# Latent value products of twelve heads as three products of rounded and remaining parts, with the values moved behind the scores, and a token scale and an entry reordered

## The chip, the core and the metric

The kernel runs on one core of one Trainium2 chip. The metric is the device time of one execution in microseconds (us). Engines: PE (TensorE: MATMUL, with its weight loads shown as PEld), DVE (VectorE), ACT (ScalarE), POOL (GpSimd), SP (SyncE, which issues the DMAs). Each works through its own queue in order; semaphores join them.

## What is computed

A transformer of three layers over 512 tokens of width 1024, in float32. The first layer mixes gated linear attention, sliding-window attention and causal pooling, then a feed-forward block. The second has a causal attention of 16 heads of 64 ("fox") and a feed-forward block. The third has latent attention of 16 heads of 128 ("mla") and a feed-forward block. The change touches the token scale at the entry of fox, and latent attention, cut here to what matters:

```python
def mla_shared_kv(x, kv_in_g, w_dkv, kv_norm_g, w_uk, w_uv, cos, sin):
    ckv = rmsnorm_2(x, kv_in_g) @ w_dkv
    latent = rmsnorm_2(ckv[..., :KV_LORA], kv_norm_g)          # 256 wide
    k_rope = apply_rope(ckv[..., KV_LORA:], cos, sin)
    k_nope = (latent @ w_uk).reshape(b, s_len, MLA_HEADS, 128)
    v = (latent @ w_uv).reshape(b, s_len, MLA_HEADS, 128)

def mla_mixer(h, w_dq, q_norm_g, w_uq, w_out, k_nope, k_rope, v, cos, sin):
    q = (rmsnorm_2(h @ w_dq, q_norm_g) @ w_uq)                 # 768 -> 16 x (128 + 64)
    ...
        sc = (qn . k_nope + qr . k_rope) * scale               # masked by chunks of 64 tokens
        p = jax.nn.softmax(sc, axis=-1)
        return jnp.einsum('bhqk,bkhd->bqhd', p, v)             # the value product of the title
    return o.reshape(b, s_len, 16 * 128) @ w_out
```

## The kernel before

**Weights.** All weights come as 380 chunks of up to 8 blocks of 128 columns. SP fetches chunk c into slot c mod 4 once PE has finished chunk c-4 (`fetch`, L539). ACT rounds it to fp32r (`casts`, L1276, WHI), POOL subtracts to get the remainder (L595, WLO), and PE makes each product of three passes of fp32r: WHI with the rounded input, WHI with the remainder of the input, WLO with the rounded input (`split_mm`, L603 to L605; by tokens `token_part`, L688 to L690). `part` and `group` run such a product into one PSUM bank. `bank_free` makes the first matmul of a group wait until the group that had the bank before was drained by DVE (semaphore `drained`).

**Order.** Each engine's order is written out by hand: the same step (`mla_pair`, `fox_pair`) stands once in the PE block, once in ACT's and once in DVE's. `linear_plan` gives the order of the chunks, and `bank_table` derives the banks from it, two banks taking turns for most groups.

**A latent pair p** (heads a = 2p and b = 2p+1, for p = 0 to 6). PE: scores of a and b (`mla_scores`, L1163 masks and L1173 products); `qr.p+1` (rotary queries) and `qn.a+2` (queries), 18 matmuls each; `turn` of a (10 transposes, L1053); for p > 0 the values `mv` (24 matmuls of 256 columns); the keys `kn.a+2` and `kn.b+2` (6 matmuls each); `mla_weigh` of a (L1062: probabilities by values, in full fp32, over 512, 384, 256 and 128 columns); turn of b; `qn.b+2`; weigh of b. ACT: the exponentials, the casts, the copy of the turned probabilities to MPT (`copy_turned`, L1561), the rounded parts of queries and keys, the rounded output. DVE: row maxima and scaling of the probabilities (L2167, L2178); the rope, that is the drain of `qr` to QRS, RT, four TURNED and the sum RT (L1752, L1749, L2345); the drain of `qn.a+2` to QNF; those of values and keys; the remainders; the output's remainder.

**Entry of latent attention.** PE: `kn.0`, `kn.1`, the sum of squares for the query norm (`stats("qn", 6)`, L712), `qr.0`, `qn.0`, `qn.1`, `mv0`, then the pairs.

**Token scales.** `stats` multiplies ones with SUMSQ over 512 columns (L712) and ACT makes RSTD by Ln and Exp (`root`). Two sites (`mixpost`, `ffnpost`) do otherwise: `token_sums` (L717, matmuls of 1 column), a square root of 4 columns on ACT (`deviation`), a reciprocal on DVE, and `spread` (L724) with filling matmuls (`keep_clock`, L731) around it. Fox has `stats` in the middle of its value products (before the third row block of k = 6), `root`, and a turn of RSTD to columns (`by_token_scale`, L758), after which DVE drains FV.

## Time and profile before

| | |
|---|---|
| median of 3 runs | 2189.12 us (2186.57 to 2189.54) |
| the profiled execution: its time | 2188.44 us |
| its span | 2186.6 us (1.8 us lie around it) |
| PE, PEld busy | 2166.6 (99%), 1774.1 (81%) |
| DVE, ACT, POOL busy | 1218.9 (56%), 898.5 (41%), 967.9 (44%) |
| mean granted clock of TensorE | 0.997 of full speed |
| DMA | 191.76 MB, 27.9% of 16 engines |

Busy times are sums over the whole span. A matmul's duration includes the time it takes to drain; what one costs in a stream is the distance from its start to the next one's. "idle before, releaser" gives how long an engine stood still before an instruction, and whose end let it go.

### The profile page before, as it was taken

The page shows a single profiled execution, that of the slowest core. Times are in us where ns is not written, and L with a number is a line of the kernel's source. Part 1 is how long each engine was busy: PE and PEld are TensorE (multiplying, and loading weights), DVE is VectorE, ACT ScalarE, POOL GpSimd, SP SyncE. Part 2 cuts the span into 40 slices and gives each one's busy share as a digit, 9 for nine tenths or more (in the row PEclk, how much of TensorE's full clock was granted, in tenths as well). Part 3 has the DMA queues.
Part 4 walks back from the last instruction along what each step waited for, and adds up shares of the span by engine and source line. Part 5 has one row for each costly group of instructions (what it writes and reads, how often), then busy time and mean ns, then how long its engine had stood idle before and what let it go on. Part 6 is the DMA issues. An engine that isn't in the chain of part 4 may idle for free.

```text
span 2186.6 us, 26205 instructions
## 1 busy us (share of the span) xinstructions
PE 2166.6 (99%) x10422; PEld 1774.1 (81%) x10422; DVE 1218.9 (56%) x1713; ACT 898.5 (41%) x1406; POOL 967.9 (44%) x741
## 2 busy tenths in 40 slices
PE   9999999999999999999999999999999999999998
PEld 6887788878888887777888888887888888888887
DVE  4975424478995136775566661177666425666511
ACT  5224422354343234675533332265444434333322
POOL 4434335545565444321554444444222344444442
PEclk9999999999999999999999999999999999999999
DMA  5222222323333323111333323332111133333332
GB/s 183 78 68 68 73 83 95 104 90 97 97 97 93 98 76 99 60 57 58 97 97 97 97 94 97 99 94 68 56 54 54 58 106 97 97 97 97 94 98 89
DMA packets 59097, 191.76 MB, mean 88 GB/s; under 512 B 6592, under 2 KB 8800, under 8 KB 58976
## 3 DMA queue, kind: packets, MB, share of 16 engines
q1 hardware_dynamic: 58976, 190.09, 27.9%
q8 instruction: 83, 1.36, 0.3%
q14 instruction: 38, 0.31, 0.0%
HBM read 187.96 MB, written 2.10 MB: 87 GB/s over the span
## 4 chain that ended last, share of the span: by engine, by line
PE 92%; DVE 5%; ACT 1%; DMA 1%; issue 1%; SPq 0%; DVEq 0%; ACTq 0%
PE ps L603 26%; PE ps L604 26%; PE ps L605 26%; PE ps L1173 2%; PE ps L1062 1%; PE ps L1053 1%; PE ps L688 1%; PE ps L689 1%; PE ps L690 1%; DVE TURNED L1749 1%; PE ps L1122 1%; DMA RAW<-weights 1%; PE ps L1091 1%; PE ps L780 1%; DVE SUMSQ L1765 1%
## 5 line engine op out<-in xcount | busy, mean ns | idle before, releaser
L595 POOL TENSOR_TENSOR WLO<-RAW,WHI 128x512 fp32r<-128x512 f32 (+1 forms) x733 | 966.3, 1343 | 1185.0 <-ACT WHI L1276 1183.0
L1276 ACT ACTIVATE WHI<-RAW 128x1024 fp32r<-128x1024 f32 (+3 forms) x379 | 374.1, 989 | 683.9 <-DMA RAW<-weights 486.5
L603 PE MATMUL ps<-HH,WHI 128*128 128x512 f32 x1194 | 470.7, 394 | 0.0
L604 PE MATMUL ps<-HL,WHI 128*128 128x512 f32 x1194 | 465.0, 389 | 0.0
L605 PE MATMUL ps<-HH,WLO 128*128 128x512 f32 x1194 | 465.0, 389 | 0.0
L1752 DVE SCALAR_TENSOR_TENSOR CV<-U,PAR,CV 128x512 f32<-128x512 f32 x264 | 301.9, 1161 | 27.0 <-ACT CV L1524 22.0
L603 PEld LDWEIGHTS ps<-HH,WHI 128*128 128x128 f32 x1194 | 224.3, 188 | 50.9 <-issue 3.8
L604 PEld LDWEIGHTS ps<-HL,WHI 128*128 128x128 f32 x1194 | 224.3, 188 | 47.9 <-issue 2.2
L605 PEld LDWEIGHTS ps<-HH,WLO 128*128 128x128 f32 x1194 | 224.2, 188 | 46.8
L603 PE MATMUL ps<-ACTH,WHI 128*128 128x512 f32 (+1 forms) x550 | 209.4, 381 | 0.0
L604 PE MATMUL ps<-ACTL,WHI 128*128 128x512 f32 (+1 forms) x550 | 209.3, 381 | 0.0
L605 PE MATMUL ps<-ACTH,WLO 128*128 128x512 f32 (+1 forms) x550 | 209.3, 381 | 0.0
L1749 DVE TENSOR_TENSOR U<-ps,RSTD 128x512 f32<-128x512 f32 x132 | 89.0, 686 | 176.6 <-PE ps L605 164.5
L2137 DVE TENSOR_TENSOR X<-X,ps 128x512 f32<-128x512 f32 x31 | 21.2, 685 | 226.1 <-PE ps L605 226.1
L1524 ACT ACTIVATE CV<-U,PAR 128x512 f32<-128x512 f32 x132 | 106.3, 807 | 88.2 <-DVE U L1749 88.2
L603 PE MATMUL ps<-HUH,WHI 128*128 128x512 f32 x352 | 137.3, 390 | 0.0
L605 PE MATMUL ps<-HUH,WLO 128*128 128x512 f32 x352 | 137.0, 389 | 0.0
L604 PE MATMUL ps<-HUL,WHI 128*128 128x512 f32 x352 | 136.9, 389 | 0.0
L605 PEld LDWEIGHTS ps<-ACTH,WLO 128*128 128x128 f32 x550 | 103.4, 188 | 19.9
L603 PEld LDWEIGHTS ps<-ACTH,WHI 128*128 128x128 f32 x550 | 103.4, 188 | 19.9
L604 PEld LDWEIGHTS ps<-ACTL,WHI 128*128 128x128 f32 x550 | 103.4, 188 | 19.5
L1765 DVE TENSOR_TENSOR SUMSQ<-SUMSQ,SQ 128x512 f32<-128x512 f32 x77 | 74.1, 962 | 19.9 <-ACT SQ L1310 19.3
(344 smaller groups left out, 3260.1 us busy)
## 6 DMA issues: line engine op xcount, KB each, us to landing
RAW<-weights SPq DMA_DIRECT2D x288, 512.0 KB, 3.5
RAW<-weights SPq DMA_DIRECT2D x56, 384.0 KB, 3.0
RAW<-weights SPq DMA_DIRECT2D x29, 256.0 KB, 2.6
RAW<-weights SPq DMA_DIRECT2D x8, 320.0 KB, 2.9
outT<-X SPq DMA_DIRECT2D x8, 256.0 KB, 2.2
X<-xT SPq DMA_DIRECT2D x3, 512.0 KB, 8.5
X<-xT SPq DMA_DIRECT2D x2, 256.0 KB, 4.0
RESET<-resets SPq DMA_DIRECT2D x1, 512.0 KB, 9.4
```

The costliest lines, as they stand in the source:

```text
L595: pool.tensor_tensor(WLO[:, slot, w], RAW[:, slot, w], WHI[:, slot, w].bitcast(F32), ALU.subtract).then_inc(w_lo, 1)
L603: pe.matmul(out, wh, hh, start=first, stop=False)
L604: pe.matmul(out, wh, hl, start=False, stop=False)
L605: return pe.matmul(out, wl, hh, start=False, stop=last)
L688: pe.matmul(o, hi[k][:, q], WHI[:, slot, w], start=k == 0, stop=False)
L689: pe.matmul(o, lo[k][:, q], WHI[:, slot, w], start=False, stop=False)
L1173: mm = pe.matmul(ps[:, 2 + 3 * odd + bank, col:col + length], q_[:, i * P:(i + 1) * P], k_[:, 0:length], start=False, stop=m == len(produc ...
L1276: act.activation(WHI[:, slot, 0:cols], RAW[:, slot, 0:cols], ACT.Copy).then_inc(w_hi, 1)
L1524: act.activation(CV[:, m, :], U[:, m, 2:2 + T], ACT.Identity, bias=par(f"conv{f}", at + 3), scale=par(f"conv{f}", at + 2)).then_inc(tap, 1)
L1749: return dve.tensor_tensor(out, a, b, ALU.mult)
L1752: return dve.scalar_tensor_tensor(out, a, scalar, b, op0, op1)
L1765: dve.tensor_tensor(SUMSQ[:, :], SUMSQ[:, :], SQ[:, slot, :], ALU.add).then_inc(sumsq, 1)
```

## The change

It does five things. (1) For pairs 0 to 5 (SPLIT_PAIRS = 6, heads 0 to 11) the value product is `split_weigh`: for the first three key blocks three fp32r passes (MVH with MPTH, MVL with MPTH, MVH with MPTL), for the last one an fp32 product (MPTF with MV). ACT writes MPTH and MPTF in the place of MPT, and MVH once a pair (`values_hi`); DVE subtracts MVL once a pair (`values_lo`) and MPTL once a head (`turned_lo`). (2) The values `mv` of pairs 1 to 6 move from behind turn(a) to behind the scores, on all engines; they get a chunk of their own, so that a pair has five chunks where it had four. (3) Fox gets the token scale by `token_sums`, `deviation` and `spread`, with the sums later, before the second row block of k = 7. (4) `token_sums` multiplies with 128 columns of ones in the place of one, at all its sites, and the readers take every 128th column. (5) At the entry of latent attention `qr.0` and the sum come ahead of the keys, and the rope is made before the scale is known and scaled afterwards.

```diff
@@ linear_plan
+    whole("qr.0", QLORA_K)
     add(("kn.0", "kn.0", 0, LORA_K), ("kn.1", "kn.1", 0, LORA_K))
-    for name in ("qr.0", "qn.0", "qn.1"):
+    for name in ("qn.0", "qn.1"):
         whole(name, QLORA_K)
...
         a, b = 2 * p + 2, 2 * p + 3
+        if p:
+            tokens([f"mv{p}.{half}" for half in range(2)], f"mv{p}", 0, 2 * LORA_K)
         if p < MLA_H // 2 - 1:
             whole(f"qr.{p + 1}", QLORA_K)
             whole(f"qn.{a}", QLORA_K)
-        values = [(f"mv{p}.{half}", f"mv{p}", 0, 2 * LORA_K, 0) for half in range(2)] if p else []
...
+            add((f"kn.{a}", f"kn.{a}", 0, LORA_K), (f"kn.{b}", f"kn.{b}", 0, LORA_K))
             whole(f"qn.{b}", QLORA_K)
@@ PE
-                    mm = pe.matmul(ps[:, bank, col + n:col + n + 1], squares[:, b * P:(b + 1) * P], ones[:, 0:1],
+                    mm = pe.matmul(ps[:, bank, col + n * P:col + (n + 1) * P], squares[:, b * P:(b + 1) * P], ones,
...
-                    if k == KD - 2 and r == 2:
-                        stats("fox", 8)
+                    if k == KD - 1 and r == 1:
+                        pe.wait_ge(sumsq, SQ_AT["fox"] + KD + 2)
+                        token_sums(7, 0, SUMSQ, range(NT), True, True).then_inc(stat_done, 1)
...
-                        by_token_scale("fox")
+                        pe.wait_ge(inverted, 1 + SITES_BY_TOKEN.index("fox"))
+                        spread(7, range(NT)).then_inc(rstd_done, 1)
...
+            def split_weigh(n):
+
+                out, own = ps[:, 4 + 3 * (n % 2), :], slice(n % 2 * P, n % 2 * P + P)
+                pe.wait_ge(a_pt, (n + FOX_H) * 3 + 3)
+                pe.wait_ge(mv_lo, n // 2 + 1)
+                pe.wait_ge(turned_lo_done, n + 1)
+                for j in range(NT - 1):
+                    bank, col, length = COLS[j]
+                    at = slice(bank * T + col, bank * T + col + length)
+                    pe.matmul(out[:, j * P:T], MVH[:, j, own], MPTH[:, at], start=j == 0, stop=False)
+                    pe.matmul(out[:, j * P:T], MVL[:, j, own], MPTH[:, at], start=False, stop=False)
+                    pe.matmul(out[:, j * P:T], MVH[:, j, own], MPTL[:, at], start=False, stop=False)
+                pe.matmul(out[:, (NT - 1) * P:T], MV[:, NT - 1, own], MPTF[:, :], start=False, stop=True).then_inc(a_o, 1)
@@ mla_pair on PE
                 mla_scores(b)
+                if p:
+                    mla_values(p)
                 group(f"qr.{p + 1}", *CQ_)
                 group(f"qn.{a + 2}", *CQ_)
                 mla_turn(a)
-                if p:
-                    mla_values(p)
                 group(f"kn.{a + 2}", *L_)
                 group(f"kn.{b + 2}", *L_)
-                mla_weigh(a)
+                weigh_head(a)
@@ ACT
-            root("fox", D, RSTD)
+            deviation("fox", D, 7)
             casts(chunk_of("fv1.0", 2))
+            act.wait_ge(rstd_done, STAT_AT["fox"] + 1)
+            act.activation(RSTD[:, :], ps[:, 7, :], ACT.Copy).then_inc(row_done, 1)
...
+            def values_hi(p):
+                product(f"mv{p}.1")
+                act.activation(MVH[:, 0:NT - 1, :], MV[:, 0:NT - 1, :], ACT.Copy).then_inc(mv_hi, 1)
@@ DVE
+            def values_lo(p):
+                dve.wait_ge(mv_hi, p + 1)
+                dve.tensor_tensor(MVL[:, 0:NT - 1, :], MV[:, 0:NT - 1, :], MVH[:, 0:NT - 1, :].bitcast(F32), ALU.subtract
+                                  ).then_inc(mv_lo, 1)
+            def turned_lo(n):
+
+                for b, length in enumerate((T, 3 * P, 2 * P)):
+                    dve.wait_ge(a_pt, (n + FOX_H) * 3 + b + 1)
+                    at = slice(b * T, b * T + length)
+                    last = dve.tensor_tensor(MPTL[:, at], ps[:, 2 + 3 * (n % 2) + b, 0:length], MPTH[:, at].bitcast(F32),
+                                             ALU.subtract)
+                last.then_inc(turned_lo_done, 1)
@@ mla_pair on DVE
                 rotated(p + 1)
+                if p < SPLIT_PAIRS:
+                    values_lo(p)
                 drain_q(a + 2)
-                if p:
-                    drain_values(p, 0)
-                    drain_values(p, 1)
+                if p < SPLIT_PAIRS:
+                    turned_lo(a)
                 drain_k(a + 2)
@@ entry on PE and on DVE
-            pe.wait_ge(lat_done, LORA_K)
+            group("qr.0", *CQ_, (lat_done, LORA_K))
+            pe.wait_ge(col_read, 2)
+            stats("qn", 6)
             group("kn.0", *L_)
             group("kn.1", *L_)
-            pe.wait_ge(col_read, 3)
-            stats("qn", 6)
-            group("qr.0", *CQ_, (lat_done, LORA_K))
...
+            dve.tensor_scalar(QRS[:, :], ps[:, BANK["qr.0"], :], MLA_SCALE, None, ALU.mult).then_inc(drained, 1)
...
+            rope(dve.tensor_tensor(RT[:, :], TURNED[:, :], RT[:, :], ALU.add))
```

In a pair of the first six the order now is, on PE, scores a and b, mv, qr, qn, turn(a), kn twice, weigh(a), turn(b), qn, weigh(b). How the instructions stand at the three places that matter is shown here (names as in the program; x is a count, waits are semaphores).

PE, the first value product of pair 1 (heads 2 and 3), before:

```order
L605 MATMUL ps<-LH,WLO 128x512
L1062 MATMUL ps<-MPT,MV 128x512 [waits a_pt,drained]
L1062 MATMUL ps<-MPT,MV 128x384
L1062 MATMUL ps<-MPT,MV 128x256
L1062 MATMUL ps<-MPT,MV 128x128
L1053 MATMUL ps<-CON,MP 128x128 [waits a_p]
```

and now:

```order
L616 MATMUL ps<-LH,WLO 128x512
L1208 MATMUL ps<-MPTH,MVH 128x512 [waits turned_lo_done,mv_lo,a_pt]
L1209 MATMUL ps<-MPTH,MVL 128x512
L1210 MATMUL ps<-MPTL,MVH 128x512
L1208 MATMUL ps<-MPTH,MVH 128x384
L1209 MATMUL ps<-MPTH,MVL 128x384
L1210 MATMUL ps<-MPTL,MVH 128x384
L1208 MATMUL ps<-MPTH,MVH 128x256
L1209 MATMUL ps<-MPTH,MVL 128x256
L1210 MATMUL ps<-MPTL,MVH 128x256
L1211 MATMUL ps<-MPTF,MV 128x128
L1064 MATMUL ps<-CON,MP 128x128 [waits a_p]
```

Four fp32 products became nine fp32r products and one fp32 product, and they wait for two more semaphores, both counted up by DVE.

DVE, pair 1, from the drain of the rotary queries on, before:

```order
L1752 SCALAR_TENSOR_TENSOR QRS<-ps,RSTD 128x512 [waits lin_done,m_rot]
L1749 TENSOR_TENSOR RT<-QRS,CS 128x512 [waits drained]
L1749 TENSOR_TENSOR TURNED<-QRS,CS 32x512 x4
L2345 TENSOR_TENSOR RT<-TURNED,RT 128x512 [waits m_dve]
L1752 SCALAR_TENSOR_TENSOR QNF<-ps,RSTD 128x512 [waits lin_done]
L1749 TENSOR_TENSOR MV<-ps,RCOL 128x512 [waits lin_done] x2
L1749 TENSOR_TENSOR KNF<-ps,RSTDK 128x512 [waits lin_done] x2
L2352 TENSOR_TENSOR QRHL<-RT,QRHL 64x512 [waits rope_hi]
L2352 TENSOR_TENSOR QRHL<-RT,QRHL 64x512
```

and now:

```order
L1802 SCALAR_TENSOR_TENSOR QRS<-ps,RSTD 128x512 [waits lin_done,m_rot]
L1799 TENSOR_TENSOR RT<-QRS,CS 128x512 [waits drained]
L1799 TENSOR_TENSOR TURNED<-QRS,CS 32x512 x4
L2397 TENSOR_TENSOR RT<-TURNED,RT 128x512 [waits m_dve]
L2413 TENSOR_TENSOR MVL<-MV,MVH 128x768 [waits mv_hi]
L1802 SCALAR_TENSOR_TENSOR QNF<-ps,RSTD 128x512 [waits lin_done]
L2421 TENSOR_TENSOR MPTL<-ps,MPTH 128x512 [waits a_pt]
L2421 TENSOR_TENSOR MPTL<-ps,MPTH 128x384 [waits a_pt]
L2421 TENSOR_TENSOR MPTL<-ps,MPTH 128x256 [waits a_pt]
L1799 TENSOR_TENSOR KNF<-ps,RSTDK 128x512 [waits lin_done] x2
L2404 TENSOR_TENSOR QRHL<-RT,QRHL 64x512 [waits rope_hi]
L2404 TENSOR_TENSOR QRHL<-RT,QRHL 64x512
```

The two drains of MV are gone from here (they stand behind the row maxima now); MVL stands ahead of the drain to QNF, and three MPTL stand ahead of the drains to KNF.

PE, the keys of the same pair, now (before, the second group waited for `mv1.1`, which DVE drains after QNF):

```order
L614 MATMUL ps<-LH,WHI 128x512 [waits w_lo,drained]
L615 MATMUL ps<-LL,WHI 128x512
L616 MATMUL ps<-LH,WLO 128x512
L614 MATMUL ps<-LH,WHI 128x512
L615 MATMUL ps<-LL,WHI 128x512
L616 MATMUL ps<-LH,WLO 128x512
L614 MATMUL ps<-LH,WHI 128x512 [waits drained]
L615 MATMUL ps<-LL,WHI 128x512
L616 MATMUL ps<-LH,WLO 128x512
L614 MATMUL ps<-LH,WHI 128x512
L615 MATMUL ps<-LL,WHI 128x512
L616 MATMUL ps<-LH,WLO 128x512
```

The first row of the second group waits for `drained`, and by the table of banks the group that had this bank is `qn.4`, whose drain is the QNF above.

## Rows read from the trace of the kernel before

**Rows 1.** The page: engines, and one group of weight loads

```profile
PE 2166.6 (99%) x10422; PEld 1774.1 (81%) x10422; DVE 1218.9 (56%) x1713; ACT 898.5 (41%) x1406; POOL 967.9 (44%) x741
...
L603 PEld LDWEIGHTS ps<-HH,WHI 128*128 128x128 f32 x1194 | 224.3, 188 | 50.9 <-issue 3.8
```

**Rows 2.** PE's timeline at mixpost's and fox's sums: start us, us, engine, line, operation

```profile
435.15 0.95 PE L717 MATMUL ps<-CON,SUMSQ 128*128 128x1 f32 x8
...
830.71 0.39 PE L690 MATMUL ps<-WLO,HH 128*128 128x512 f32 x1
833.25 1.28 PE L712 MATMUL ps<-SUMSQ,CON 128*128 128x512 f32 x2 [2.15 <-DVE SUMSQ L1765]
...
842.75 1.05 PE L758 MATMUL ps<-CON,RSTD 1*128 1x1 f32 x8
```

**Rows 3.** Windows, three stretches: busy us, then granted clock, DMA share, GB/s

```profile
834.10:837.30 3.20, 3.20 (x8) 2.32 (x7) 0.00 (x0) 3.17 (x3) 2.70 (x3) 0.50 0.01 3
438.30:441.60 3.30, 3.30 (x13) 1.87 (x12) 1.80 (x4) 0.23 (x1) 0.00 (x0) 0.51 0.00 0
1492.70:1494.30 1.60, 0.00 (x0) 0.00 (x1) 1.60 (x2) 1.49 (x2) 1.60 (x2) 1.00 0.31 101
```

**Rows 4.** PE's timeline at the entry of latent attention

```profile
1476.45 1.10 PE L712 MATMUL ps<-SUMSQ,CON 128*128 128x512 f32 x2 [0.77 <-DVE SUMSQ L1765]
...
1494.30 0.29 PE L1163 MATMUL ps<-M 128*128 128x64 bf16 x4 [1.60 <-DVE QNL L2322]
```

**Rows 5.** The chain that ended last, one value product (start us, us)

```profile
1639.59 2.16 PE ps L1062 x8
```

**Rows 6.** PE's timeline, scores of a latent head

```profile
1559.53 0.40 PE L1173 MATMUL ps<-KRL,QRHL 128*128 128x512 f32 x1
1559.76 0.34 PE L1173 MATMUL ps<-KNH,QNH 128*128 128x384 f32 x1
1559.94 0.34 PE L1173 MATMUL ps<-KNH,QNL 128*128 128x384 f32 x1
...
1561.21 0.28 PE L1173 MATMUL ps<-KNH,QNL 128*128 128x256 f32 x1
1561.33 0.28 PE L1173 MATMUL ps<-KNL,QNH 128*128 128x256 f32 x1
```

**Rows 7.** PE's timeline in pair 0: turn(a), kn.a, kn.b, weigh(a)

```profile
1509.05 1.25 PE L1053 MATMUL ps<-CON,MP 128*128 128x128 f32 x10
1510.06 0.48 PE L603 MATMUL ps<-LH,WHI 128*128 128x512 f32 x1
...
1511.97 0.50 PE L603 MATMUL ps<-LH,WHI 128*128 128x512 f32 x1 [0.27 <-DVE QNF L1752]
...
1513.47 1.02 PE L1062 MATMUL ps<-MPT,MV 128*128 128x512 f32 x2
```

**Rows 8.** Timelines of DVE, POOL, ACT and PE in pair 3

```profile
1628.58 0.69 DVE L1752 SCALAR_TENSOR_TENSOR QRS<-ps,RSTD 128x512 f32<-128x512 f32 x1 [0.94 <-PE ps L605]
...
1632.82 1.66 DVE L2345 TENSOR_TENSOR RT<-TURNED,RT 128x512 f32<-128x512 f32 x1
1634.40 0.68 DVE L1752 SCALAR_TENSOR_TENSOR QNF<-ps,RSTD 128x512 f32<-128x512 f32 x1
...
1632.44 2.64 POOL L595 TENSOR_TENSOR WLO<-RAW,WHI 128x512 fp32r<-128x512 f32 x2 [10.80 <-ACT WHI L1276]
...
1631.52 0.85 ACT L1276 ACTIVATE WHI<-RAW 128x768 fp32r<-128x768 f32 x1 [5.49 <-DMA RAW<-weights]
1633.03 1.36 ACT L1561 ACTIVATE MPT<-ps 128x512 f32<-128x512 f32 x3 [0.67 <-PE ps L1053]
...
1632.39 1.25 PE L1053 MATMUL ps<-CON,MP 128*128 128x128 f32 x10
```

**Rows 9.** The page: DMA issues, KB each, us to landing

```profile
RAW<-weights SPq DMA_DIRECT2D x56, 384.0 KB, 3.0
RAW<-weights SPq DMA_DIRECT2D x29, 256.0 KB, 2.6
```

More of the change, by code:

```diff
@@ L165, in linear_plan @@
             whole(f"qn.{a}", QLORA_K)
-        values = [(f"mv{p}.{half}", f"mv{p}", 0, 2 * LORA_K, 0) for half in range(2)] if p else []
-        if p < MLA_H // 2 - 1:
-            values += [(f"kn.{n}", f"kn.{n}", 0, LORA_K, (4 + 2 * (n - a)) * P) for n in (a, b)]
-        chunks.append(values)
-        if p < MLA_H // 2 - 1:
+            add((f"kn.{a}", f"kn.{a}", 0, LORA_K), (f"kn.{b}", f"kn.{b}", 0, LORA_K))
             whole(f"qn.{b}", QLORA_K)
@@ L408, in on_chip_model @@
         TURNED = nc.alloc_sbuf_tensor_at("TURNED", [P, T], F32, offset=sumsq_at)
+        mpt_at = mol_at + MLA_H * T * 4
+        MPTH = over("MPTH", [P, 5 * 2 * P], mpt_at, F32R)
+        MPTL = over("MPTL", [P, 5 * 2 * P], mol_at + 2 * SPLIT_PAIRS * T * 4, F32R)
+        MPTF = over("MPTF", [P, P], mol_at + (2 * SPLIT_PAIRS + 3) * T * 4)
+        MVH = over("MVH", [P, NT, 2 * P], hh_at + 2 * SPLIT_PAIRS * T * 4, F32R)
+        MVL = over("MVL", [P, NT, 2 * P], hh_at + (2 * SPLIT_PAIRS + 2) * T * 4, F32R)
         CKV = nc.alloc_sbuf_tensor_at("CKV", [P, LORA_K, T], F32, offset=mol_at)
@@ L500, in on_chip_model @@
         SITES = list(STAT_AT)
-        SITES_BY_TOKEN = ("mixpost", "ffnpost")
+        SITES_BY_TOKEN = ("mixpost", "ffnpost", "fox")
         def par(name, at=0, n=1):
@@ L1499, in _ @@
                 fb_square("wout", j, "mixpost")
-            deviation("mixpost", D)
+            deviation("mixpost", D, 6)
             for j in range(KD):
@@ L1537, in _ @@
             casts(chunk_of("fv0.0", 2))
-            deviation("ffnpost", D)
+            deviation("ffnpost", D, 6)
             for j in range(KD):
@@ L1644, in _ @@
                 square(j, (SQ_AT["qn"] + j) % 2, CQ[:, j, :], "qn")
+            casts(chunk_of("qn.1"))
             root("qn", QLORA_K * P, RSTD)
+            casts(chunk_of("mv0.0"))
             def query_hi(n):
@@ L1706, in _ @@
             key_hi(1)
-            casts(chunk_of("mv0.0"))
             rotated_hi(0)
@@ L2179, in normalise @@
                 last.then_inc(a_p, 1)
-            scale_known("fox")
-            col_scale(2)
+            dve.wait_ge(ln_done, STAT_AT["fox"] + 1)
+            dve.reciprocal(RCOL[:, :], RCOL[:, :]).then_inc(inverted, 1)
+            dve.wait_ge(inverted, 1 + SITES_BY_TOKEN.index("fox"))
             for r in range(NT):
                 drain_rows(f"fv0.{r}", FV[:, r, 0:512], r, RCOL)
+            dve.wait_ge(row_done, 1)
             drain("foxf", FZ[:, 0, :])
@@ L2361, in mla_softmax @@
                     row_maxima(2 * p + h + FOX_H, h, 2 + 3 * h)
+                if p:
+                    drain_values(p, 0)
+                    drain_values(p, 1)
                 for h in range(2):
@@ L2384, in mla_pair @@
                 head_out(b)
+            dve.wait_ge(lin_done, DONE["qr.0"])
+            dve.tensor_scalar(QRS[:, :], ps[:, BANK["qr.0"], :], MLA_SCALE, None, ALU.mult).then_inc(drained, 1)
+            dve.wait_ge(drained, DRAIN["qr.0"])
+            mul(RT[:, :], QRS[:, :], CS[:, 0, :])
+            dve.wait_ge(stat_done, STAT_AT["qn"] + 1)
+            rope(swapped(TURNED, range(4)))
+            rope(dve.tensor_tensor(RT[:, :], TURNED[:, :], RT[:, :], ALU.add))
             scale_known("kvn")
@@ L2389, in _ @@
             scale_known("qn")
-            drain_rope(0)
-            rope(swapped(TURNED, range(4)))
-            rotated(0)
+            mul(RT[:, :], RT[:, :], RSTD[:, :]).then_inc(m_rot, 1)
             drain_q(0)
+            key_lo(0)
+            key_lo(1)
+            rotated_lo(0)
+            query_lo(0).then_inc(head_ready, 1)
             drain_q(1)
-            rotated_lo(0)
-            key_lo(0)
-            query_lo(0).then_inc(head_ready, 1)
-            key_lo(1)
             query_lo(1).then_inc(head_ready, 1)
```

37 lines of the change are left out of this document (30 added, 7 removed).

## The prediction

> **What bounds the kernel now.** I read the page first: PE is busy 99% of the span [rows 1]. So the time is the length of PE's queue plus the few places where PE stands still or runs at the lower clock, and a change is worth what it takes from that queue less what it makes PE wait. Next I read PE's own rows for its waits and the windows for the granted clock. Three places stand out. At the end of fox's first value half, the row block before ends, then the sum over SUMSQ waits 2.15 us for DVE [rows 2], and right behind it the granted clock is 0.50, that is 1.2 in place of 2.4 GHz, for 3.2 us [rows 3]. Another stretch at 0.51 follows the one-column matmuls of the mixpost site [rows 3]. The entry of latent attention has waits of 0.77 and 1.60 us [rows 4]; there the clock stayed at 1.00 [rows 3]. In the latent pairs PE hardly waits; what matters there is how much room DVE has, so last I read the rows of DVE, ACT and POOL in one pair.
>
> The sum is made against the profiled execution, 2188.4 us; the median of the runs, 2189.1, is 0.7 above.
>
> **The passes.** A value product takes 2.16 us of PE [rows 5]. In a stream, start to start, an fp32r pass costs 0.23 us over 512 columns, 0.18 over 384 and 0.12 over 256 [rows 6]. Three of each are 1.59, and the fp32 product over 128 of the 1280 columns, a tenth of 2.16, is 0.22: 1.81, or about 1.9 with the start of a new stream. That is 0.3 us less a head, 0.6 a pair, and 3.6 for twelve heads.
>
> **What waits for the new parts.** Count from the start of turn(a). The turn takes 1.01 and each key group 1.5 or less: in pair 0 the turn starts at 1509.05, kn.a at 1510.06, and kn.b at 1511.97 because it waits for QNF, and weigh starts 1.50 later [rows 7]. Without that wait a key group is six passes of 0.23, 1.4, so kn.b could begin at 2.4 and weigh(a) at 3.8. Now look at DVE in pair 3, where turn(a) starts at 1632.39: QRS starts 3.8 earlier, the sum of the rope ends at 2.1, QNF at 2.7 [rows 8]. Before, PE covered this with the values, some 3.1 us of work between turn and keys. They have moved away, and kn.b now waits for QNF in every pair, as in pair 0.
>
> Ahead of QNF stands MVL, 768 columns from SBUF. No row has it: the least is 0.69, a subtraction of 512, the most 1.04, that in proportion; I take 1.0. Behind QNF stand three MPTL of 512, 384 and 256 columns: 0.69 and in proportion 0.52 and 0.35, together 1.5 to 1.6. ACT is no limit: MPT was complete 2.0 after the turn's start [rows 8], and one more small copy makes that 2.3.
>
> How late the rope ends depends on POOL. The rope's last step took 1.66 us where POOL's WLO was running, against the 0.69 of QRS before it. QNF, which reads PSUM, took 0.68 beside the same WLO [rows 8]. In pair 3 the rope was held once, by 0.97; without that it ends at 1.1. Now two chunks come at it. The values free their chunk 8.0 before turn(a) (36 passes of 0.23 lie between), the 384 KB take 3.0 [rows 9], the cast 0.85 [rows 8], and POOL starts near -4.1, one us ahead of RT: I price this hold at 0.8. The rotary queries end at -3.95, their successor is now the 256 KB of the next values, 2.6 [rows 9] and a cast of 0.6, so POOL starts near -0.65, in the middle of TURNED: 1.0. The rope ends at 2.9, MVL at 3.9, QNF at 4.6, kn.b starts at 4.65 and ends at 6.0, MPTL is there at 6.15. Weigh(a) starts at 6.2 in place of 3.8: **a wait of 2.4 us in each of pairs 1 to 5**, against 0.6 gained. The bounds: no hold at all gives QNF at 2.8 and MPTL at 4.4, a wait of 0.6; holds of 1.0 and 1.5 give 3.1. I take 2.4, by the times at which the two chunks land.
>
> The Trainium skill (SBUF — State Buffer, "SBUF: two separate sides") says that a DVE operation with two SBUF inputs and a GpSimd operation that reads SBUF exclude each other for a whole instruction. By that rule MVL, with two SBUF inputs, can be held by a third piece of WLO as well, and the five pairs would be up to 5 us longer; the three MPTL, with one input in PSUM, could not. The trace agrees as far as it goes: 1.66 for the first kind, 0.68 for the second.
>
> Pair 0 has its values ahead of the pairs, so only the second hold: rope 2.1 to 2.5, weigh(a) at 5.7, while before it was at 4.4 [rows 7]: +1.3, less 0.6, is +0.7. Pairs 1 to 5: 5 x (2.4 - 0.6) = +9.0. Pair 6 has no new parts but the new order: QNF at 3.6, kn.b 1.2 late: +1.2. Weigh(b) has room: turn(b) and qn.b are 5.2 us of cover behind weigh(a), in which DVE has five drains and remainders of 0.7, the output's remainder and 1.6 for MPTL; I cost it at nothing, and if this cover is gone it is up to 0.8 a pair. The last pair is as before.
>
> **Clock in the pairs.** PE stands still in front of kn.b from 2.4 to 4.65, 2.25 us. The nearest rows are the wait of 2.15 that was followed by 1.2 GHz and the one of 1.60 that was not [rows 2, 3, 4]. A fall that lasts 3.2 us costs 1.6. Five such waits: none to five falls, 0 to 8 us. I take one, 1.6: the wait of 2.15 had its fall, but a single row doesn't make it a rule for all five.
>
> **Fox.** The sum moves behind k = 6 and the first row block of k = 7. That is twelve more passes, 2.7 us, and DVE's last square let the sum go 2.3 after the block before it: the wait goes, with 0.4 to spare, and with it the low clock behind it. From 830.94, where the next pass would have started, to 842.75 the rows show 11.81 us [rows 2]. The work in it is 30 passes of 0.2275 and the sum, 2.16 x 512 / 1280 = 0.86, together 7.7. So **-4.1 us**. The sum itself keeps its size (four fp32 products of 128 columns for one of 512). Spread, eight matmuls of 128 columns, takes the place of the turn to columns, eight of 1 column; both are 0.8 to 1.0 by the rows of the next part. The square root, the reciprocal and ACT's copy of the row lie beside fv1; DVE's drains begin earlier than before, so nothing is late there.
>
> **Mixpost, ffnpost, final.** Four fp32 products of 1 column, eight matmuls, took 0.95 [rows 2]; ten transposes of 128 columns take 1.01 [rows 7], so eight matmuls of 128 are 0.8 and a little, the same within 0.1. But behind the one-column groups at mixpost the clock was 0.51 for 3.3 us, half of which is 1.65 lost [rows 3]. With full columns in that stretch I expect the clock to hold. Since PE may then wait for its first input tile, I take -1.0 (0 to -1.65). The final site adds 0.1.
>
> **Entry.** Putting qr.0 first lets the last squares finish under it, and the rope starts 4.7 us earlier and no longer holds up the first head. Both waits of rows 4 go, 0.77 + 1.60. The first pass stood at 1472.8 (twelve passes end where the wait of 0.77 begins). The longest chain left is qn.0 (48 passes and the sum later, 1484.6), QNF, the rounded part, two KNL, two QRHL, QNL, 4.5 us, against the end of mv0 at 1491.9: cover 2.7, by which even two holds fit. **-2.4.**
>
> **Sum.** Fox -4.1, mixpost -1.0, final +0.1, entry -2.4, pairs +0.7 +9.0 +1.2, clock +1.6: +5.1, so 2193.5 against the profiled time and **2194 against the median**. A measurement of this kernel can tell about 0.2%, 4.4 us, from no change.
>
> **Rivals.**
> - *DVE is in time* (faster). If WLO misses the rope, weigh(a) waits 0.6 at most, the pairs give nothing away, and the gains outside remain: -7.4 and -1 at most, 2180 to 2182. It decides at MPTL complete 3.8 to 4.4 us after the turn starts. For it: in pair 3 QRS, RT and TURNED ran unheld, and only the last step met WLO. Against: the chunk that the values free is timed to land just ahead of RT. 14%.
> - *One hold a pair* (no change): a wait of 1.4, pairs +4 to +5, total -3: 2185 to 2188. The case if a landing is 0.8 us earlier or later than I reckon. 26%.
> - *The clock falls in most pairs*, or MVL is held too (slower): 8 us for five falls in place of 1.6, or 5 for MVL: 2199 to 2203. 15%.
> - *The passes aren't cheaper*, because each has its own weight load of 0.188 [rows 1] and costs no less: then 384 and 256 columns cost 0.19, a product 2.1, and the gain of 3.6 goes. The rows show 0.12 for passes with a new weight each [rows 6], so I give it 3% and leave it in the range.
> - My forecast has 42%, with a range of its own of 2189 to 2199.
>
> **How the numbers follow.** The range of 2181 to 2203 leaves out the lower half of the first rival and a little above the third. Faster by over 0.2% is below 2184.7: the first rival and a part of the second, 0.20. Within 0.2%: the rest of the second and the lower part of the forecast, 0.34. Slower: 0.46.
>
> **What would show it.** PE's row of kn.b in each of the first seven pairs should have an idle time before it that ends with QNF, 1 to 3 us; weigh(a) should follow MPTL; TURNED or RT should be longer than 0.69 in most pairs. Value products should take 1.8 to 1.9. Fox's sum should start without a wait, with a clock of 1.00 behind it, and the stretch behind mixpost's sums should be at 1.00 too. The first scores should follow mv0 at once. The forecast is wrong if kn.b starts within 1 us of kn.a's end, or if mixpost's clock stays low.

## The result and the profile after

The changed kernel takes 2190.1 us (median of 20 runs, 2188.1 to 2191.8) where the kernel before took 2187.1 in the same comparison (20 runs, 2185.2 to 2191.2). The ratio is 1.0013 with a 95% interval of 1.0007 to 1.0019: 3 us slower, inside the predicted range, and less than the 5 of the forecast. By the bound of 0.2% that the prediction set, it counts as no change, which had 0.34; slower by more than that had 0.46.

The engines on the page of the profiled execution (span 2188.4, against 2186.6 before) answer to [rows 1]; the second block is PE's waits over the latent pairs (line waited at, releaser: us in total, times, longest):

```profile
PE 2161.8 (99%) x10464; PEld 1777.3 (81%) x10464; DVE 1246.3 (57%) x1756; ACT 902.7 (41%) x1429; POOL 966.9 (44%) x740
```

```profile
PE ps L614 <- DVE QNF L1802: 11.4, 7, 2.4
PE ps L1176 <- DVE MOL L2408: 1.4, 2, 0.8
PE ps L1208 <- DVE MPTL L2421: 0.7, 1, 0.7
```

PE is busy 4.8 us less and the program is longer all the same. The seven waits at L614 are kn.b in the first seven pairs. A wait costs some 0.3 more than the idle time shown: in pair 2 the value product starts 5.70 after the turn, and with nothing to wait for (experiment 11) 3.84, which is 1.86 later for an idle time of 1.57. The idle time is counted from the drained end of the last pass, and the first pass of a new stream takes longer. PE's timeline in pair 2 shows one of them, and a split value product behind it:

```profile
1566.65 1.26 PE L1064 MATMUL ps<-CON,MP 128*128 128x128 f32 x10
...
1568.90 0.39 PE L616 MATMUL ps<-LH,WLO 128*128 128x512 f32 x1
1570.86 0.50 PE L614 MATMUL ps<-LH,WHI 128*128 128x512 f32 x1 [1.57 <-DVE QNF L1802]
...
1572.35 0.47 PE L1208 MATMUL ps<-MPTH,MVH 128*128 128x512 f32 x1
...
1574.22 1.26 PE L1064 MATMUL ps<-CON,MP 128*128 128x128 f32 x10
```

The product takes 1.87 from its start to that of the next turn, against 2.16 before [rows 5]. DVE and POOL in the same stretch:

```profile
1562.83 0.69 DVE L1802 SCALAR_TENSOR_TENSOR QRS<-ps,RSTD 128x512 f32<-128x512 f32 x1 [0.69 <-PE ps L616]
1563.56 0.81 DVE L1799 TENSOR_TENSOR RT<-QRS,CS 128x512 f32<-128x512 f32 x1
1564.38 4.22 DVE L1799 TENSOR_TENSOR TURNED<-QRS,CS 32x512 f32<-32x512 f32 x4
1568.64 0.69 DVE L2397 TENSOR_TENSOR RT<-TURNED,RT 128x512 f32<-128x512 f32 x1
1569.25 0.95 DVE L2413 TENSOR_TENSOR MVL<-MV,MVH 128x768 fp32r<-128x768 f32 x1
1570.12 0.68 DVE L1802 SCALAR_TENSOR_TENSOR QNF<-ps,RSTD 128x512 f32<-128x512 f32 x1
1570.72 1.48 DVE L2421 TENSOR_TENSOR MPTL<-ps,MPTH 128x512 fp32r<-128x512 f32 x3
...
1562.53 2.43 POOL L606 TENSOR_TENSOR WLO<-RAW,WHI 128x512 fp32r<-128x512 f32 x2 [11.56 <-ACT WHI L1303]
1566.08 1.28 POOL L606 TENSOR_TENSOR WLO<-RAW,WHI 128x512 fp32r<-128x512 f32 x1 [1.12 <-ACT WHI L1303]
```

DVE goes without a gap from QRS to the last MPTL. Two pieces of POOL's work lie on it: the first stretches RT and one TURNED step, the second another TURNED step, so that the four take 4.22. QNF comes 4.15 after the turn's start, kn.b at once behind it, and the value product at 5.7, right after the third MPTL (1572.20).

Windows of the granted clock, to be read against [rows 3] (us, busy times, then clock, DMA share, GB/s): behind mixpost's sums, at fox's sum, and behind kn.b in pair 4.

```profile
434.90:442.40 7.50, 7.05 (x42) 4.75 (x42) 4.49 (x8) 2.10 (x4) 0.77 (x2) 1.00 0.16 52
829.00:842.00 13.00, 13.00 (x67) 11.03 (x66) 8.60 (x13) 5.48 (x8) 9.02 (x8) 1.00 0.41 122
1637.30:1640.70 3.40, 3.40 (x10) 2.65 (x11) 2.89 (x6) 2.00 (x6) 1.10 (x2) 0.59 0.02 4
```

Both low stretches of before are gone, and a new one stands behind the longest wait, 2.39 us in pair 4. The first scores of the latent stage start at 1485.62 instead of 1494.30 [rows 4]: **8.7 us gained by then**, about 2.6 of it because the trace of before has the two low stretches (experiment 1). The scores of the last pair start at 1713.41 instead of 1711.65: **the pairs took 10.4 back**. From scores to scores the seven pairs before the last cost +0.8, +1.8, +1.2, +1.9, +3.1, +1.3 and +0.3.

### The profile page after: what moved, and what is told of

Read it like the earlier page. It is cut to its first block, busy times and chain, and to the rows that moved or that the text cites. A ratio compares the mean times of both kernels' runs of the same rounds, so it can differ in the third digit from the quotient of the medians.

```text
span 2188.4 us, 26359 instructions
## 1 busy us (share of the span) xinstructions
PE 2161.8 (99%) x10464; PEld 1777.3 (81%) x10464; DVE 1246.3 (57%) x1756; ACT 902.7 (41%) x1429; POOL 966.9 (44%) x740
## 4 chain that ended last, share of the span: by engine, by line
PE 93%; DVE 4%; DMA 1%; ACT 1%; issue 0%; SPq 0%; POOL 0%; DVEq 0%; ACTq 0%
PE ps L614 26%; PE ps L616 26%; PE ps L615 26%; PE ps L1186 2%; PE ps L699 1%; DVE TURNED L1799 1%; PE ps L700 1%; PE ps L701 1%; DMA RAW<-weights 1%; PE ps L1064 1%; PE ps L1135 1%; PE ps L1104 1%; PE ps L791 1%; PE ps L1073 0%; PE ps L865 0%
## 5 line engine op out<-in xcount | busy, mean ns | idle before, releaser
L614 PE MATMUL ps<-HH,WHI 128*128 128x512 f32 x1194 | 470.6, 394 | 0.6 <-POOL WLO L606 0.6
L614 PEld LDWEIGHTS ps<-HH,WHI 128*128 128x128 f32 x1194 | 224.2, 188 | 51.6 <-issue 3.8
L614 PE MATMUL ps<-ACTH,WHI 128*128 128x512 f32 (+1 forms) x550 | 209.5, 381 | 0.0
L614 PE MATMUL ps<-HUH,WHI 128*128 128x512 f32 x352 | 137.3, 390 | 0.0
L614 PEld LDWEIGHTS ps<-ACTH,WHI 128*128 128x128 f32 x550 | 103.4, 188 | 19.6
```

The lines of the kernel that those rows point to most:

```text
L614: pe.matmul(out, wh, hh, start=first, stop=False)
```

## The experiments

The kernels were timed in three groups of four; the median of before was 2186.2, 2187.1 and 2187.7 beside them. So each kernel is compared by its ratio to the before of its own group. A ratio's interval is about 2 us to either side (up to 3 where a kernel ran five or six times), and a difference of two ratios is less sure than that.

**1. The two parts outside the pairs, each alone.** First the fox token scale with the wide sums on the kernel before:

```
-                    if k == KD - 2 and r == 2:
-                        stats("fox", 8)
+                    if k == KD - 1 and r == 1:
+                        pe.wait_ge(sumsq, SQ_AT["fox"] + KD + 2)
+                        token_sums(7, 0, SUMSQ, range(NT), True, True).then_inc(stat_done, 1)
...
-            root("fox", D, RSTD)
+            deviation("fox", D, 7)
...
```

> The kernel before with only the change's token scale of the fox layer and its 128-column sums (the reader's view of them too); pairs and entry as before. My theory: the fox part gives 4.1 and mixpost 1.0 (one full clock instead of the throttled stretch), so 2187.1 - 5.1 = 2182 (range 2180.5 to 2184), with the granted clock 1.00 at both places. Rival, that what came out after was made elsewhere: fox sums queued later give only the matmul's own time back, under 2, and the run stands at 2185 or above.

Measured: 2182.7, ratio 0.9982 (0.9974 to 0.9991), about 4 us faster. Then the entry alone, PE's part shown (ACT's and DVE's orders follow it):

```
...
-            pe.wait_ge(lat_done, LORA_K)
+            group("qr.0", *CQ_, (lat_done, LORA_K))
+            pe.wait_ge(col_read, 3)
+            stats("qn", 6)
             group("kn.0", *L_)
             group("kn.1", *L_)
-            pe.wait_ge(col_read, 3)
-            stats("qn", 6)
-            group("qr.0", *CQ_, (lat_done, LORA_K))
...
```

> The kernel before with only the new entry of the latent stage (rotary product first, statistics behind it, queries' rest ordered anew). My theory: the waits of 0.77 and 1.60 ahead of the first scores go, so 2187.1 - 2.4 to 2.8 = 2184.5 (range 2183.3 to 2186). Rival: the gain of the entry comes only with the shorter product of the split values behind it, then the run stands at 2186.5 or above.

Measured: 2184.0, ratio 0.9989 (0.9980 to 0.9997). Its trace has no wait at the entry, and from the first pass of the stage to the first scores it takes 18.73 us (1470.16 to 1488.89), where the run with the old entry takes 21.49: 2.75 gained. It also shows something on the fox part, which is as before in this kernel. PE's row of fox's sum, and the windows behind it and behind mixpost's one-column sums:

```profile
832.30 0.70 PE L713 MATMUL ps<-SUMSQ,CON 128*128 128x512 f32 x1 [2.17 <-DVE SUMSQ L1766]
...
438.30:441.60 3.30, 2.92 (x17) 1.47 (x16) 2.26 (x5) 0.83 (x2) 0.00 (x0) 1.00 0.00 0
832.30:835.50 3.20, 3.20 (x12) 2.32 (x13) 0.00 (x0) 3.03 (x3) 3.01 (x3) 1.00 0.01 3
```

The same wait and the same one-column groups stand there, and the clock stays at 1.00. So the two low stretches of [rows 3] come in some executions and not in others. The times of before say so too: over 64 of its executions beside these runs the median is 2185.8 where the mean clock was 0.999, 2187.0 at 0.998 and 2187.9 at 0.997. At full clock the fox part alone is worth 2.7: the same pass of the stage behind it starts at 859.24 in the run with it and at 861.71 in the run without, while ahead of the sum the run with it is 0.2 behind (824.75 and 824.52). Mixpost was at full clock in both. Another 0.4 comes by the end of fox's pairs; what it comes from was not looked into.

**2. Both parts together, the pairs untouched** (the two diffs above in one kernel).

> The kernel before with both parts of the change that lie outside the pairs (fox token scale with the 128-column sums, and the latent entry), the pairs untouched. If the parts are independent: 2186.2 - 3.5 - 2.3 = 2180.4 (range 2179 to 2182), which would be below both kernels, and the change's pairs then cost the difference to the changed kernel, 9. If they overlap (the fox part's gain and the entry's both being the same clock stretch or the same wait), 2182.5 or more.

Measured: 2179.9, ratio 0.9969 (0.9958 to 0.9981), 6.8 faster. They add up (0.18% + 0.11% = 0.29%, against 0.31%). So the pairs of the changed kernel cost 0.44%, 9.6 us, in timed runs (11 by the traces, 1.5 of it the low clock in pair 4).

**3. No head split, all else as changed.**

```
-SPLIT_PAIRS = 6
+SPLIT_PAIRS = 0
```

> The changed kernel with no head's value product split: all sixteen in single fp32 passes, values still behind the scores, entry and fox changed. Theory A (the split costs DVE and GpSimd-port work in front of kn.b that eats what its passes give back): the waits ahead of kn.b stay, as the rope chain still stands there, but without the remainder of the values (0.95) and of the first turned head (1.5); they fall from 1.6 to under 0.7 a pair, and the time is 2181 to 2184, that is, below the kernel before and 6 to 9 below the changed one. Theory B (the split is a gain that the new order hides): each pair loses the 0.6 of its two cheaper products and gets no wait back: 2193 to 2195.

Measured: 2185.1, ratio 0.9995 (0.9986 to 1.0003); a point above the range of theory A and far from B. The 9.6 come apart into two: moving the values behind the scores costs 5.7 (0.9969 to 0.9995), and splitting the products costs 3.9 more (0.9995 to 1.0013). Each of the two is known to some 3 us; the traces have 6.4 and 4.5 for them, from the first scores of the stage to those of the last pair. I had expected the waits ahead of kn.b to fall below 0.7 in each pair. They are 0.6 to 1.6, and the rotary steps are still held (TURNED x4 takes 4.29 in pair 1):

```profile
PE ps L614 <- DVE QNF L1802: 6.5, 7, 1.6
```

**4. The values' remainder out of the queue.**

```
                 for h in range(2):
                     normalise(2 * p + h + FOX_H, h, MP[:, h, :])
+                if p < SPLIT_PAIRS:
+                    values_lo(p)
...
                 rotated(p + 1)
-                if p < SPLIT_PAIRS:
-                    values_lo(p)
                 drain_q(a + 2)
```

> The changed kernel with one DVE instruction moved: the remainder of the values (128x768, 0.95 us) stands behind the probabilities' scaling instead of between the rotary sum and the query's drain. In the trace of the changed kernel DVE is idle there for about 0.7 before the rotary product comes. Theory A (the length of DVE's queue from the rotary product to the query's drain sets kn.b): the waits ahead of kn.b fall by 0.7 in each of the pairs 0 to 5, from 1.5-1.8 to 0.8-1.1, and the run stands 4 to 5 below the changed kernel, at 2184 to 2186 where the kernel before has 2186. Theory B (DVE only follows TensorE, kn.b waits for something that starts with the turned head): waits and time as in the changed kernel, 2188 to 2190.

Measured: 2185.1, ratio 0.9993 (0.9984 to 1.0001). PE's waits have 8.0 at kn.b instead of 11.4, the clock is not low in the pairs, and by the ratios it is 4.4 faster than the changed kernel:

```profile
PE ps L614 <- DVE QNF L1802: 8.0, 7, 1.9
```

Theory A holds in the pairs 1 to 5: what DVE does between QRS and QNF is paid by PE. In pair 2 QNF ends 0.53 earlier after the turn's start (3.62 for 4.15), and the wait is 0.53 shorter (1.04 for 1.57). It is not the whole 0.87 that was moved: QRS starts 0.09 later, and the first hold is longer (RT takes 1.07 in place of 0.81). In pair 0 the wait did not fall (1.88 for 1.80): there DVE has no idle time ahead of QRS, so MVL pushed the rope back by what it took away behind it.

**5. The control: another consumer first.**

```
                 rotated(p + 1)
+                drain_q(a + 2)
                 if p < SPLIT_PAIRS:
                     values_lo(p)
-                drain_q(a + 2)
```

> The changed kernel with the query's drain put ahead of the remainder of the values on DVE. A control: the same instructions in the same stretch, another consumer first. Theory A with two waits in a row (kn.b for the drained query, then the first value product for the remainder of the turned head): kn.b's waits fall by 0.95, but the value product right behind it then waits about 0.8, so that the sum of the two is as before and the time within 1 of the changed kernel (2188.5 to 2190.5). Theory B (only the wait of kn.b counts): 5 to 6 below the changed kernel, 2183 to 2185.

Measured: 2189.0, ratio 1.0013 (1.0004 to 1.0022), as the changed kernel. PE's waits:

```profile
PE ps L614 <- DVE QNF L1802: 6.2, 7, 1.6
PE ps L1208 <- DVE MPTL L2421: 5.3, 11, 0.7
```

6.2 and 5.3 are 11.5 in place of 11.4 and 0.7. Most of what left kn.b went to the value product behind it, and the time stayed: in pair 2 the turn after weigh(a) starts 7.56 after the one before it, and 7.57 in the changed kernel. kn.b and this product are asked for one right behind the other and are fed by one queue, so what counts is when the queue is through with both.

**6. GpSimd off the rotary steps.** ACT makes the rounded weights, POOL their remainders behind it. Two casts move behind the turned head's copies:

```
                 if 0 < p < SPLIT_PAIRS:
                     values_hi(p)
+                mla_turned(a)
                 if p:
                     casts(chunk_of(f"mv{p}.0") + RING)
                 casts(chunk_of(f"qr.{p + 1}") + RING)
-                mla_turned(a)
```

> The changed kernel with ACT's two weight casts (of the values' chunk and of the next rotary chunk) moved behind the turned head's copies, so that GpSimd's weight remainder, which follows them, no longer falls on DVE's rotary steps. Theory A (the shared port: two holds of 0.8 to 1.0 us on the rotary steps are what makes kn.b late): rotary steps of 0.7 each instead of up to 1.7, waits ahead of kn.b of 0 to 0.6 in place of 1.5 to 2.4 in the pairs 0 to 5, time 2190.1 - 6 to 8 = 2183 (range 2182 to 2187, the upper end if the remainder then falls on the next DVE steps). Theory B (the queue alone is too long, holds are incidental): waits shorter by under 0.4 each, time 2188 to 2190. Theory C: the later casts make a weight late on TensorE, a new wait appears ahead of a qn or kn product, and the time rises above 2190.

Measured: 2202.2, ratio 1.0075 (1.0061 to 1.0089), 13.6 slower than the changed kernel by the two ratios. Theory C had the sign, but no weight is late on TensorE, and no theory had the size. PE's waits, then DVE and POOL in pair 1:

```profile
PE ps L1208 <- DVE MPTL L2421: 18.0, 6, 3.0
PE ps L1176 <- DVE MOL L2408: 0.5, 1, 0.5
```

```profile
1533.78 2.77 DVE L1799 TENSOR_TENSOR TURNED<-QRS,CS 32x512 f32<-32x512 f32 x4
...
1541.38 3.15 DVE L2404 TENSOR_TENSOR QRHL<-RT,QRHL 64x512 fp32r<-64x512 f32 x2
1544.54 1.00 DVE L2374 TENSOR_TENSOR QNL<-QNF,QNH 128x384 fp32r<-128x384 f32 x1
1545.46 2.92 DVE L2384 TENSOR_TENSOR KNL<-KNF,KNH 128x512 fp32r<-128x512 f32 x2
1548.31 0.68 DVE L2408 TENSOR_TENSOR MOL<-ps,MOH 128x512 fp32r<-128x512 f32 x1
1548.91 1.47 DVE L2421 TENSOR_TENSOR MPTL<-ps,MPTH 128x512 fp32r<-128x512 f32 x3
...
1539.04 8.80 POOL L606 TENSOR_TENSOR WLO<-RAW,WHI 128x512 fp32r<-128x512 f32 x7 [20.96 <-ACT WHI L1303]
```

The first half of theory A is right. TURNED x4 takes 2.77 instead of 4.22, and no idle time is left ahead of kn.b in any of the seven pairs. But POOL now works in one block of 8.80, and beside it stand other steps with two operands in SBUF. QRHL x2, QNL and KNL x2 took 1.39, 0.56 and 1.28 in the changed kernel; here they take 3.15, 1.00 and 2.92, 3.8 more. The steps that read PSUM beside the same block (MOL, MPTL) keep their length. The second head's MPTL stands behind all of them, and the second value product waits 3.0 in six pairs. The clock was then low at four of the six waits, 17.1 us in all; I reckon half of it, 8.5, as lost (a little less, as 0.8 of it lies in a wait). A window over the product in pair 1:

```profile
1550.50:1554.00 3.50, 3.48 (x15) 3.14 (x16) 1.03 (x2) 1.15 (x2) 1.27 (x1) 0.53 0.00 0
```

The sum: 18.5 of waits and 8.5 of clock, less the changed kernel's 13.5 of waits and 1.7 of clock, is 11.8. The spans differ by 12.0 (2200.4 and 2188.4). The sum is rough by about 1, as each wait costs a little more than its idle time.

**7. One head's remainder moved in front of three steps.** On top of the late casts:

```
                 rotated_lo(p + 1)
                 query_lo(a + 2)
+                if p < SPLIT_PAIRS:
+                    turned_lo(b)
                 key_lo(a + 2).then_inc(head_ready, 1)
                 key_lo(b + 2)
                 head_out(a)
-                if p < SPLIT_PAIRS:
-                    turned_lo(b)
```

> The run with late casts and one edit more: the second turned head's remainder ahead of both keys' remainders on DVE; the values' remainder stays where the change put it. Theory A (the 3.0 ahead of the second value product was one step of the queue standing behind two keys' remainders of 1.8 and 1.2 and the first head's output of 0.7): the wait falls to under 0.8 and with it the clock falls that came after it, time 2176 to 2180 against 2202 with late casts alone. Theory B (both edits of the reordered kernel were needed): above 2185.

Measured: 2176.1, ratio 0.9952 (0.9939 to 0.9964). That is in theory A's range. No value product waits, and no low clock is left in the pairs. By the two ratios 27 us hung on where one head's remainder stood, some 18 of waits and 8 of clock.

**8. The same with the values' remainder early as well** (the edits of 4, 6 and 7 together).

> The run with late casts (2202.2) had no wait ahead of kn.b, but 3.0 ahead of the second value product, whose operand stood on DVE behind six remainders of operands that GpSimd's weight remainder now slowed. This kernel keeps the late casts, and on DVE puts the values' remainder behind the probabilities' scaling and the second turned head's remainder ahead of both keys' remainders and of the first head's output. Theory A (one DVE queue, GpSimd's holds fall on whatever two-SBUF-operand step stands beside them, what counts is whether TensorE's operand is in front of it or behind): both waits go, under 0.5 each pair is left, time 2202 - 6 times 2.6 to 3.0 = 2184 to 2187, about the kernel before or just below. Theory B (DVE is out of time in a pair of 33 us whatever the order): the wait comes back ahead of the next scores, and the time stays above 2192.

Measured: 2175.6, ratio 0.9952 (0.9940 to 0.9965), 8.4 below the near end of theory A's range: I had priced the waits that go, and not the 8.5 of low clock that stood behind them. Left are 1.6 us of waits for the first head's output and 0.3 for one MPTL. Against experiment 7 the early remainder of the values adds nothing that these runs can tell. The traces show why: in pair 2 turn(a), both key groups and weigh(a) are through in 5.63 in place of 5.98, because QNF ends at 1.81 and not at 2.58, where kn.b had to wait for it a little; and qn.b with weigh(b), in front of scores that wait for MOL, gives the 0.35 back (6.50 in place of 6.14).

**9. Is it the order alone?** Edits 4 and 7, but the casts as the change has them:

> The reordered kernel without the late casts: values' remainder and second turned head's remainder early on DVE, ACT's casts where the change has them, so that GpSimd's weight remainder falls on the rotary steps again. Theory A (the holds on the rotary steps set kn.b): the waits of 0.9 to 1.3 ahead of kn.b stay as in the run with the early remainder of the values (2185.1), time 2184 to 2186. Theory B (the order on DVE is all, the holds matter nowhere once it is right): 2176 to 2179.

Measured: 2184.0, ratio 0.9986 (0.9977 to 0.9995), with 8.2 us of waits ahead of kn.b (8.0 in experiment 4):

```profile
PE ps L614 <- DVE QNF L1802: 8.2, 7, 1.8
```

The holds on the rotary steps matter by themselves: 0.34%, 7.4 us, lie between this and the reordered kernel. The two edits work only as a pair: the late casts alone lose 13.6, and the second head's remainder alone gains nothing that these runs can tell (0.9993 and 0.9986, whose intervals overlap; 0.5 us by the traces of the pairs).

**10. What the three passes are worth.** The reordered kernel with SPLIT_PAIRS = 0:

> The reordered kernel (2175.6) with no head split: twelve value products go back to one fp32 pass each. It asks what the three passes are worth where TensorE waits for nothing. Theory A (0.3 less a product): no wait appears, turned head to turned head is 0.3 longer than in the split kernel, time 2175.6 + 12 x 0.3 = 2179.2 (range 2178 to 2181). Theory B (the three passes give nothing by themselves, all of the gain came with the order): 2175 to 2176.5.

Measured: 2177.2, ratio 0.9956 (0.9944 to 0.9968), less than theory A's 2179.2. Part of that is the 1.6 us of waits that only the split kernel has; experiment 11, where they are gone too, is 3.8 us below this kernel. Not all of it is the split's: by the traces 3.1 us lie in the six split pairs and 0.7 in pair 6, whose products are not split in either, and where this kernel waits 0.47 for ACT's MPT. From turn to turn a pair takes 30.99 us without the split and 30.48 with it (1530.57 to 1561.56, and 1530.78 to 1561.26), 0.5 for two products.

**11. The last waits.**

```
                 key_lo(a + 2).then_inc(head_ready, 1)
-                key_lo(b + 2)
                 head_out(a)
+                key_lo(b + 2)
                 drain_q(b + 2)
```

> The reordered kernel with the first head's output remainder ahead of the second key's remainder on DVE. Its seven waits of 0.15 to 0.43 (1.6 in all) ahead of the scores, which stood for that output, should go in the pairs 0 to 5: 2175.6 - 1.0 = 2174.6. If the wait only moves to the key's remainder, 2175.6 as before.

Measured: **2173.5**, ratio 0.9937 (0.9925 to 0.9949): 13.8 us faster than the kernel before and 16.6 faster than the change, by the ratios. It is more than the 1.0 that I had expected: by the traces of the pairs 2.7, because an idle time of 0.16 stood for a delay of 0.3, and pair 6 lost another delay of 0.6. Against the kernel with untouched pairs (experiment 2) it is 7 us less by the ratios, 5.8 by the traces. The engines on its page, its only wait in the pairs, and DVE and POOL in pair 2:

```profile
PE 2158.0 (99%) x10464; PEld 1776.6 (82%) x10464; DVE 1249.9 (58%) x1756; ACT 898.2 (41%) x1429; POOL 972.0 (45%) x740
```

```profile
PE ps L1208 <- DVE MPTL L2421: 0.2, 1, 0.2
```

```profile
1556.66 0.95 DVE L2413 TENSOR_TENSOR MVL<-MV,MVH 128x768 fp32r<-128x768 f32 x1
...
1558.95 2.77 DVE L1799 TENSOR_TENSOR TURNED<-QRS,CS 32x512 f32<-32x512 f32 x4
...
1562.97 1.48 DVE L2421 TENSOR_TENSOR MPTL<-ps,MPTH 128x512 fp32r<-128x512 f32 x3
...
1566.56 3.06 DVE L2404 TENSOR_TENSOR QRHL<-RT,QRHL 64x512 fp32r<-64x512 f32 x2 [0.57 <-ACT QRHL L1693]
...
1570.56 1.47 DVE L2421 TENSOR_TENSOR MPTL<-ps,MPTH 128x512 fp32r<-128x512 f32 x3
...
1564.12 8.37 POOL L606 TENSOR_TENSOR WLO<-RAW,WHI 128x512 fp32r<-128x512 f32 x7 [17.20 <-ACT WHI L1303]
```

DVE is as busy as in the changed kernel, and the holds are about as long as in experiment 6 (QRHL x2 takes 3.06, there 3.15). They fall where PE has its 18 query passes and a value product as cover, and what PE asks for first now stands first.

## Why the prediction came out as it did

**The mechanism held.** The forecast said that kn.b would wait for QNF in every pair, behind a rope that WLO holds twice, with MVL and MPTL in the same queue. Each link is in the rows of pair 2. Taking MVL out of the queue shortened the waits (4), which consumer DVE served first made no difference (5), and with the holds off the rope kn.b had no idle time ahead of it (6), whereas with DVE's order right and the holds left on the rope it waited 8.2 us (9). The prices in the experiments were not all right: without the split the time stood above its range (3), and in 6 the holds landed where nobody had priced them.

**The sizes, term by term.** Times from the turn's start:

| step | forecast | measured |
|---|---|---|
| rope ends | 2.9 | 2.7 in pair 2 (two holds), 3.5 in pair 4 |
| QNF ends | 4.6 | 4.15, 4.96 |
| last MPTL | 6.15 | 5.55, 6.36 |
| kn.b and weigh(a), nothing waiting | 2.4 and 3.8 | 2.48 and 3.84 (experiment 11) |
| weigh(a), as changed | 6.2 | 5.70 in pair 2 |
| delay of the value product or of kn.b, pairs 1 to 5 | 2.4 | 1.8 to 2.0, once 2.5 (idle time 1.5 to 1.8, once 2.4) |
| MVL | 1.0 | 0.95 |
| three MPTL | 1.5 to 1.6 | 1.48 |
| a value product | 1.9 | 1.87 (weigh(a)), 1.79 (weigh(b)) |

The term that was mis-sized is the wait in the pairs, by 0.5 in pair 2 (weigh(a) at 5.70 for 6.2), and it is all in DVE's queue (MPTL ready at 5.55 for 6.15): the first hold was 0.57 (RT 0.12 and a TURNED step 0.45) where I took 0.8, and from one start to the next MVL takes 0.87 and QNF 0.60, less than the durations that I added up. The floor was right. The three MPTL were done during kn.b's six passes, so kn.b's wait was the whole of it and the value product came straight behind.

**Pairs 1 to 5** cost 9.3 by the trace, the clock's share in it, against 9.0 and 1.6 forecast. The delays at kn.b come to 10.7 (forecast 12.0), the low clock to 1.5 (1.6), the cheaper products to -3.2 (-3.0). Two terms had been left out. The 24 passes of the values run shorter behind the scores (2.88 from start to start) than behind the turn (2.95 to 3.29 in the trace of before): -1.3. And weigh(b), which I cost at nothing, waited once (0.7), and the scores twice for MOL (0.6 and 0.8), the output's remainder that stands behind more work now: +1.6 against the same places before, where the scores had waited 0.3 once. That these two nearly cancel is luck. Pair 0 was +0.8 (forecast +0.7). **Pair 6** was +0.3 where I had said +1.2: kn.b and weigh(a) came 1.0 late and not 1.2, the values' passes gave 0.4, and weigh(b) and the passes ahead of it another 0.3.

**The clock in the pairs.** One fall was forecast and one came, behind the longest wait. That was a choice between none and five, and the runs don't turn it into a rule (below).

**Fox and mixpost.** -5.1 was forecast and the traces differ by 5.9 at the start of the latent stage (1472.80 and 1466.88): 4.3 right behind fox's sum (forecast 4.1), 0.8 at mixpost (1.0), 0.6 in the pairs of fox and 0.2 at the very start. That is closer than the reasoning deserved, for the prediction treated the low clock behind fox's wait and behind mixpost's sums as belonging to them. Experiment 1 shows both without it. At full clock fox is worth 2.7 (and 0.4 in its pairs), mixpost nothing or close to it, and the two together gained 0.18% over many executions, some of which had low stretches and some not. The step that failed is "with full columns in that stretch I expect the clock to hold": it held with one column as well (entry alone), though not in the trace of before. Nor does the fox sum keep its size, as I had said: it takes 0.81 from its start to the next pass, where the sum over 512 columns took 0.56 (entry alone).

**Entry.** -2.4 forecast, -2.75 measured; the waits went whole, and the cover was enough.

**The total.** By the timed ratios the parts outside the pairs gave 6.8 (forecast 7.4) and the pairs cost 9.6 (forecast 12.5, the clock in it), so it is the pairs that made the forecast 2 us too long: by the traces 1.3 in the delays of pairs 1 to 5 and 0.9 in pair 6.

**The rivals.** "DVE is in time" is excluded by the waits. "One hold a pair" came near in the total (its range ended at 2188), but not in the mechanism, for there were two holds. "The passes aren't cheaper" is excluded by experiments 10 and 11. The prediction did not see the largest fact of the case: the gain that it counted for the passes, 3.6, is there (3.1 in the split pairs), and 13 us more stood behind two orders (experiment 7), ACT's casts and the second head's remainder on DVE, which the change had left where they stood.

On the exclusive port, the Trainium skill (SBUF — State Buffer, "SBUF: two separate sides") says that a DVE step with two SBUF inputs and a GpSimd step that reads SBUF exclude each other for a whole instruction. The runs agree, with QRHL at 0.7 free and 1.45 and 1.68 held (experiment 6), and MPTL, with one input in PSUM, at 1.47 or 1.48 for the three in either case. The third hold, on MVL, which that rule made possible, never came (0.95 in all six pairs); no piece of WLO was running when an MVL started, so the runs do not test it.

## What to carry to other kernels

When two engines exclude each other, moving the work of one may only move the hold, so put it where the consumer has cover. In experiment 6 the holds left the rotary steps and came back on five others. Before moving it, list what will stand beside it and who waits for that: the same edit lost 13.6 us by itself, and gained 7.4 once two remainders stood elsewhere (experiments 8 and 9). And put the producer's queue in the order in which the consumer asks for its results: swapping two that are asked for close together (experiment 5) changed nothing, while moving one head's remainder in front of three steps that have time was worth 27 us beside the late casts (experiment 7), and nothing clear without them (experiment 9).
